# An MoE decoder trunk: experts' rows scattered to two rows per token and read back by plain loads

## The reference, cut to what matters

```
g_sel = argmax(g_logits)
e_in  = e_logits[token, g_sel]
top_v, top_i = top_k(e_in, 2)
top_w = softmax(top_v) * p_g
y     = sum over the two experts of top_w * (silu(x @ w_gate) * (x @ w_up)) @ w_down
x     = x + y
```

## Time and profile before

| | |
|---|---|
| median of 3 runs | 1473.19 us (1470.67 to 1476.38) |
| the profiled execution | 1473.54 us |
| its span, first to last instruction | 1471.9 us |
| PE busy | 1217.6 us (83%) |
| DVE, ACT, POOL busy | 371.1, 246.6, 230.0 us |
| moved by DMA | 350.99 MB, mean 238 GB/s |
| mean granted TensorE clock | 0.918 of full speed |

### The profile page before, as it was taken

How to read it: one execution, slowest core, us unless ns; L and a number is a source line. 1 busy time by engine, 2 the same in 40 slices (tenths; PEclk the granted TensorE clock), 3 DMA queues, 4 the chain that set the end, 5 groups by cost and what they waited for, 6 DMA issues and landing times.

```text
span 1471.9 us, 15943 instructions
## 1 busy us (share of the span) xinstructions
PE 1217.6 (83%) x6119; PEld 653.3 (44%) x6119; DVE 371.1 (25%) x808; ACT 246.6 (17%) x571; POOL 230.0 (16%) x288
## 2 busy tenths in 40 slices
PE   6999998888879689878855999997969679988770
PEld 4765574556534433333323764444734433333220
DVE  4132003544301511111114400112610531111115
ACT  2000005652201201100003201014410301000001
POOL 2300003222100011111022000303810011111103
PEclk9999999999999789989986999999969879999995
DMA  8320665749965669999948130302156659999955
GB/s 274 98 66 21 237 285 167 213 163 367 315 235 232 231 252 421 421 420 420 414 170 281 57 105 16 129 0 80 44 193 282 236 183 418 420 421 421 418 205 207
DMA packets 107725, 350.99 MB, mean 238 GB/s; under 512 B 21662, under 2 KB 40290, under 8 KB 84986
## 3 DMA queue, kind: packets, MB, share of 16 engines
q1 hardware_dynamic: 89880, 304.43, 54.1%
q0 software_dynamic: 17472, 45.37, 8.7%
q10 hardware_dynamic: 290, 0.07, 0.0%
HBM read 320.09 MB, written 44.41 MB: 248 GB/s over the span
## 4 chain that ended last, share of the span: by engine, by line
PE 58%; SPq 14%; DMA 8%; DVE 6%; issue 5%; POOL 4%; ACT 3%; POOLq 2%; DVEq 0%; ACTq 0%; PEldq 0%
SPq L1032 10%; PE ps L1222 9%; PE ps L1155 8%; PE ps L1726 8%; PE ps L436 4%; DMA moe_gu<-in_moe_w_up 4%; SPq L1054 4%; PE ps L1240 4%; PE ps L414 4%; PE ps L1677 4%; DMA fox_arena<-in_cache_k 2%; PE ps L355 2%; PE ps L694 1%; PE ps L1212 1%; PE ps L712 1%
## 5 line engine op out<-in xcount | busy, mean ns | idle before, releaser
L1222 PE MATMUL ps<-moe_gu,rows 128*64 128x512 f32 x1024 | 251.4, 648 | 58.3 <-DMA moe_gu<-in_moe_w_up 53.6
L1222 PEld LDWEIGHTS ps<-moe_gu,rows 128*64 128x64 f32 x1024 | 82.3, 149 | 204.9 <-issue 196.8
L1155 PE MATMUL ps<-moe_gu,turned 128*128 128x512 f32 x256 | 115.1, 613 | 12.4 <-DMA moe_gu<-in_fox_w_out 7.1
L1726 PE MATMUL ps<-mwblk,turned 128*128 128x512 f32 x256 | 111.5, 593 | 2.3 <-DVE vaug L1919 1.5
L1116 POOL DMA_INDIRECT expert_rows<-turned,moe_dst_row x32 | 32.0, 999 | 392.2 <-ACT turned L1327 384.6
L1494 DVE TENSOR_TENSOR turned<-turned,ps 128x256 f32<-128x256 f32 x32 | 13.5, 421 | 308.9 <-ACT turned L1317 308.9
L1155 PEld LDWEIGHTS ps<-moe_gu,turned 128*128 128x128 f32 x256 | 50.3, 198 | 76.2 <-issue 63.1
L1240 PE MATMUL ps<-moe_wd,moe_rowsel 128*64 128x512 f32 x352 | 80.4, 598 | 2.3 <-ACT turned L1327 2.3
L1726 PEld LDWEIGHTS ps<-mwblk,turned 128*128 128x128 f32 x256 | 48.0, 190 | 61.1 <-issue 57.4
L1317 ACT ACTIVATE turned<-ps 128x256 f32<-128x256 f32 x32 | 12.3, 383 | 318.0 <-PE ps L1222 318.0
L355 PE MATMUL ps<-turned,fox_arena 128*128 128x288 f32 x256 | 63.1, 407 | 0.0
(11 more groups left out here) (345 smaller groups left out, 1475.3 us busy)
## 6 DMA issues: line engine op xcount, KB each, us to landing
moe_gu<-in_moe_w_gate SPq DMA_DIRECT2D x56, 1024.0 KB, 22.7
moe_gu<-in_moe_w_up SPq DMA_DIRECT2D x56, 1024.0 KB, 24.3
moe_wd<-in_moe_w_down SPq DMA_DIRECT2D x44, 1024.0 KB, 23.0
rows<-in_moe_w_down SPq DMA_DIRECT2D x20, 1024.0 KB, 22.5
fox_arena<-in_cache_k SPq DMA_DIRECT2D x32, 512.0 KB, 7.7
fox_arena<-in_cache_v POOLq DMA_DIRECT2D x32, 512.0 KB, 9.5
fox_arena<-in_fox_w_in SPq DMA_DIRECT2D x6, 2048.0 KB, 10.1
expert_rows<-x SPq DMA_DIRECT2D x6, 2048.0 KB, 22.8
```

The source lines that it names most:

```text
L1155: mm = pe.matmul(ps[:, 2 * n + half, :], turned[:, c, n * P:(n + 1) * P], w[:, c, half * 512:half * 512 + 512], start=(c == 0), stop=(c == ...
L1222: mm = pe.matmul(ps[h, 2 + p % 2, :].rearrange("s (k f) -> s k f", k=2), xT[:, c, h], gu[s][:, half, :, c, :], start=(c == 0), stop=(c == ...
L1726: mm = pe.matmul(ps[:, m % 4, :], turned[:, c, n * P:(n + 1) * P], wblk[:, k % 3, c, :], start=(c == 0), stop=(c == KC - 1))
```

## The change

- `expert_rows` now has two rows per token (1,152 instead of 3,200). The destination of a pick is row 2 × token + j, j being 0 or 1. The fill is nine loads of 128 rows.
- The selection is in two passes. The first, for the experts' own tiles, compares the rank itself with the slot numbers (`rowsel`) and uses the one-hots over experts times the token's number, and times 2 × token + j, as `tilesel`; both are ready without floor, scan and sums. PE's ten pairs of products (32 columns) wait for all of them at once. One DVE instruction turns the result into source and destination rows (`row`). The second pass computes `tl` and `md` as before, for the 18 overflow tiles alone, with ten pairs of products (18 columns) and `more_row`. On PE it stands ahead of `turn_rows(0)`; on DVE it stands between `row` and `keep_turned(0)`.
- The one-hots of groups are no longer masked by `valid`; the products of ones for the last tile take 64 rows.
- After the experts SP waits for `scattered` and issues five plain loads, one per token tile, of two rows (8 KB) per partition, into `gu[0]` and `gu[1]`. This is still in `out_and_experts`. The ten gathers of `mlstm_project` and of `finish` are gone, and so is `slot`.
- `combine` waits for the tile's load and does both rows. In `finish` the mean of the tile before now stands behind both combinations, directly ahead of its end.
- SP's wait for six combinations ahead of the first block of projection weights is gone.

The diff, cut to its core:

```diff
@@ trunk
-        y_dram = nc.dram_tensor("expert_rows", (TILES * SLOT, D), F32, kind="Internal").ap()
+        y_dram = nc.dram_tensor("expert_rows", (2 * TOK, D), F32, kind="Internal").ap()
@@ fill_rows
+            for row in range(0, 2 * TOK, P):
+                sp.dma_start(y_dram[row:row + P, :], x[:, 0, :]).then_inc(filled, 16)
@@ out_and_experts
+            held = [gu[n // 4][:].rearrange("p h k c n -> p (h k c n)")[:, n % 4 * 2 * D:(n % 4 + 1) * 2 * D] for n in range(NT)]
@@ sp_ of out_and_experts, at its end
+                sp.wait_ge(scattered, 1)
+                for n in range(NT):
+                    sp.dma_start(held[n][0:ROWS[n], :], y_dram[2 * n * P:2 * (n * P + ROWS[n]), :].rearrange("(p j) d -> p (j d)", j=2)
+                                 ).then_inc(back_in[layer][n], 16)
@@ pool_ of out_and_experts
-                pool.wait_ge(index_ready, 2)
...
+                pool.sem_inc(scattered, 1)
@@ route
+                pe.wait_ge(sel_ready, 3)
                 for k in range(2 * NT):
-                    pe.wait_ge(sel_ready, k + 1)
                     for h in range(2):
-                        mm = pe.matmul(ps[h * SLOT:(h + 1) * SLOT, 2, 0:TILES // 2], rowsel[:, k, :], tilesel[:, k, h:TILES:2],
-                                       start=(k == 0), stop=(k == 2 * NT - 1))
+                        mm = pe.matmul(ps[h * SLOT:(h + 1) * SLOT, 2, 0:2 * STATIC].rearrange("s (u t) -> s u t", u=2), rowsel[:, k, :],
+                                       tilesel[:, k, :, h:EXP:2], start=(k == 0), stop=(k == 2 * NT - 1))
                 mm.then_inc(src_done, 1)
+                pe.wait_ge(more_ready, 1)
+                for k in range(2 * NT):
+                    for h in range(2):
+                        mm = pe.matmul(ps[h * SLOT:(h + 1) * SLOT, 3, 0:MORE].rearrange("s (u t) -> s u t", u=2), rowsel[:, k, :],
+                                       more_sel[:, k, :, h:MORE:2], start=(k == 0), stop=(k == 2 * NT - 1))
+                mm.then_inc(more_done, 1)
@@ routes
-                ch(dve.tensor_tensor(goh, goh, wide(const("valid"), GROUPS), ALU.mult))
...
-                    ch.step(dve.tensor_tensor(oh[:, j]...
+                    ch(dve.tensor_tensor(oh[:, j]...
+                dve.tensor_tensor(tilesel[:, :, 1, :], hot, back_row.broadcast_to([P, 2 * NT, EXP]), ALU.mult).then_inc(sel_ready, 1)
+                dve.tensor_tensor(tilesel[:, :, 0, :]..., oh, token.broadcast_to([P, 2, NT, EXP]), ALU.mult).then_inc(sel_ready, 1)
...
                 ch(dve.tensor_reduce(s10["r"][:], picked, AX, ALU.add))
+                dve.tensor_tensor(rowsel[:], numbers, rank.broadcast_to([P, 2 * NT, SLOT]), ALU.is_equal).then_inc(sel_ready, 1)
...
+                dve.wait_ge(src_done, 1)
+                dve.tensor_scalar(row[:].rearrange("s u t -> s (u t)"), ps[:, 2, 0:2 * STATIC], NOWHERE, None, ALU.add).then_inc(index_ready, 1)
...
+                ch.step(dve.tensor_tensor(rowsel[:], numbers, md.broadcast_to([P, 2 * NT, SLOT]), ALU.is_equal))
+                ch(dve.tensor_tensor(more_hit, ..., ALU.is_equal))
+                ch.step(dve.tensor_tensor(more_sel[:, :, 0, :]..., ALU.mult))
+                ch(dve.tensor_tensor(more_sel[:, :, 1, :], ..., ALU.mult))
+                dve.sem_inc(more_ready, 1)
...
+                dve.wait_ge(more_done, 1)
+                dve.tensor_scalar(more_row[:].rearrange("s u t -> s (u t)"), ps[:, 3, 0:MORE], NOWHERE, None, ALU.add).then_inc(index_ready, 1)
@@ combine
+        def combine(dve, layer, n, combined):
             r = ROWS[n]
+            dve.wait_ge(back_in[layer][n], 16)
+            for j in range(2):
+                if j:
+                    dve.wait_ge(combined, 2 * n + 1)
+                dve.scalar_tensor_tensor(x[0:r, n, :], back[layer][n][0:r, j * D:(j + 1) * D], share[j][0:r, n:n + 1], x[0:r, n, :], ALU.mult, ALU.add
+                                         ).then_inc(combined, 1)
@@ mlstm_project
-                sp.wait_ge(combined, 2 * NT - 4)
                 load_block(sp, 0)
...
-                for k in range(2 * NT):
-                    n, j = divmod(k, 2)
-                    gather_back(pool, yg[k][0:ROWS[n], :], n, j, yg_in[k])
@@ finish
-                for k in range(2 * NT):
-                    n, j = divmod(k, 2)
-                    gather_back(pool, yg[0:ROWS[n], k, :], n, j, yg_in[k])
...
-                    for j in range(2):
-                        k = 2 * n + j
-                        combine(dve, yg[0:ROWS[n], k, :], n, j, yg_in[k], 0, combined)
-                        if j == 0 and n:
-                            mean(dve, n - 1)
+                    combine(dve, 1, n, combined)
+                    if n:
+                        mean(dve, n - 1)
                     if n == 0:
                         dve.wait_ge(gl_in, 16)
                     else:
                         end(dve, n - 1)
```

More of the change, by code:

```diff
@@ L50 @@
           ("selpair", MPAIRS * P), ("iota_slot", SLOT), ("iota_tile", TILES),
-          ("rev4", GROUPS), ("rev32", EXP), ("token", NT), ("own_row", TILES // 2), ("valid", NT), ("minus_half", MH * NT), ("fold", LG)]
+          ("rev4", GROUPS), ("rev32", EXP), ("token", NT), ("back_row", 2 * NT), ("minus_half", MH * NT), ("fold", LG)]
 OFFSET, CW = {}, 0
@@ L89, in constants @@
     tok = np.arange(NT)[None, :] * P + i
-    c["valid"][:] = tok < TOK
     c["token"][:] = np.where(tok < TOK, tok - NOWHERE, 0)
-    c["own_row"][:] = np.arange(TILES // 2)[None, :] * P + i
+    c["back_row"][:] = np.concatenate([np.where(tok < TOK, 2 * tok + j - NOWHERE, 0) for j in range(2)], 1)
     c["minus_half"][:] = -0.5
@@ L161, in trunk @@
         half = sb("half", [P, 1])
-        slot = sb("slot", [P, 2, NT], U32)
         share = [sb(f"share{j}", [P, NT]) for j in range(2)]
@@ L181, in fill_rows @@
         def fill_rows(sp):
-            left = TILES * SLOT
-            while left:
-                n = min(left // P, NT - 1)
-                row = TILES * SLOT - left
-                sp.dma_start(y_dram[row:row + n * P, :].rearrange("(n p) d -> p n d", p=P), x[:, 0:n, :]).then_inc(filled, 16)
-                left -= n * P
+            for row in range(0, 2 * TOK, P):
+                sp.dma_start(y_dram[row:row + P, :], x[:, 0, :]).then_inc(filled, 16)
+        back_in = [[lasting(f"back_in{layer}_{n}") for n in range(NT)] for layer in range(2)]
+        back = []
         def log_sigmoid_act(act, neg_abs, e, u, lnu, bent, rounded, logged):
@@ L986, in out_and_experts @@
             both = sb(tag + "both", [P, NT + 1, EXP], where=mx)
-            c32 = {n: sb(tag + n, [P, EXP], where=mx) for n in ("ov", "end", "far")}
+            c32 = {n: wr[:].rearrange("p c s -> p (c s)")[:, 256 + k * EXP:256 + (k + 1) * EXP] for k, n in enumerate(("ov", "end", "far"))}
             rowsel = sb(tag + "rowsel", [P, 2 * NT, SLOT], where=mx)
@@ L1561, in mlstm_project @@
             HT = TOK // 2
-            vflat = vaug[:].rearrange("p n h v -> p (n h v)")
-            yg = [og[:, k, :] for k in range(NT)] + [vflat[:, k * D:(k + 1) * D] for k in range(NT)]
             hnorm = sb("hnorm", [P, D], where=small)
@@ L1583, in mlstm_project @@
             ss_done, qs_ready, gated = sem("m_ss"), sem("m_qs"), sem("m_gated")
-            combined, yg_in = sem("c0_combined"), [lasting(f"c0_yg_in{k}") for k in range(2 * NT)]
+            combined = sem("c0_combined")
             squared, meaned, rooted = sem("m_squared"), sem("m_meaned"), sem("m_rooted")
@@ L2394, in finish @@
             L = NT - 1
-            yg = sb("f_yg", [P, 2 * NT, D], where=fin)
+            sb("f_held", [P, 2 * NT, D], where=fin)
             gl = sb("gl", [P, D], where=fin)
-            combined, yg_in = sem("f_combined"), [lasting(f"f_yg_in{k}") for k in range(2 * NT)]
+            combined = sem("f_combined")
             gl_in, squared, meaned, rooted, ended, y_out = (sem("gl_in"), sem("f_squared"), sem("f_meaned"), sem("f_rooted"),
```

90 lines of the change are left out of this document (42 added, 48 removed).

## The result

| | before | after |
|---|---|---|
| median of the runs, us | 1474.22 (1470.67 to 1476.38) | 1460.50 (1458.48 to 1462.45) |
| ratio after/before, 95% interval | | 0.9913 (0.9891 to 0.9936) |
| profiled execution, its span, us | 1473.54, 1471.9 | 1459.13, 1457.4 |
| POOL: busy us, instructions | 230.0, 288 | 209.8, 268 |
| a second comparison | 1471.93 | 1460.39, ratio 0.9926 (0.9903 to 0.9950) |

The changed kernel is 13.7 us faster by the medians, 12.8 by the ratio; the second comparison gives 10.9 by its ratio and 11.5 by its medians. The forecast was 1463.9, with 1456 to 1471 as its range.

The account below looks back on a forecast made before the run. TensorE and the transfers were taken to bound the kernel in turns, the transfers inside the expert loop. From 1473.54 us, −6.3 − 5.2 − 1.6 + 3.5 = −9.6 gave 1463.9 us, range 1456 to 1471.

Parts of the forecast that it names:

- Routing: Rank product to transposes of gathered rows: transposes start 3.1 us earlier per layer, −6.3 for two layers (−4.2 to −8.0).
- Loop: Expert loop: scatters carry the same rows to other addresses and POOL issues as many, 0, bounds ±1.
- rival D: Expert loop: second selection and a slower stream eat the earlier start, loop ends as before; sum −3.3, 1470.2; chance 0.10.
- Phase end behind layer 0: After layer 0's experts: barrier earlier or later by SP's issues and POOL's drain, gate product at 788.75, −5.2 (−3.5 to −6).
- One of my signs: In the phases after the experts: no POOL instruction over 0.6 us, listed among what would show the forecast.
- POOL's drain: Projection's end and last phase's end: drain proportional to transfers POOL issued, ten gathers go, −1.6 (0 to −1.7).
- Last phase: After layer 1's experts: DVE waits for the final gain queued behind five loads, +3.5 (−3.9 to +5).
- rival B: Last phase: the gain does not stand behind the loads, −3.9 for +3.5; sum −17.0, 1456.5; chance 0.15.
- the term that was undersized: Last phase: five loads and the gain, 4.72 + 0.52 MB, take 3.73 + 4.72/0.4 = 15.5 us.
- The steps of 4.56 a tile: Last phase: each of four tiles takes two combinations, a mean, the openly awaited root and the end, 4.56 us.
- Rival C: Both phase ends after the experts: SP's drain waits for its five transfers; sum +7.5, 1481.0; chance 0.09.
- Fill: Start: row buffer's fill falls from 13.1 MB to 4.7 MB under a busy PE, 0.

Follow-up runs that it names:

- experiment 5: The kernel before with the two-pass routing alone; destinations, row buffer and gathers as before: 1463.55 us, ratio 0.9928.
- experiment 6: The changed kernel with TensorE's second selection moved behind the first expert tile's gate and up product: 1464.95 us, ratio 0.9938.
- Experiment 9: The changed kernel with the five row loads of each layer issued behind the barrier, at the start of the next phase: 1465.63 us, ratio 0.9944.
- experiment 10: The changed kernel with the final gain loaded early and the last phase's mean back between the two combinations: 1455.01 us, ratio 0.9880.
- experiment 7: The changed kernel with extra POOL drains, in each expert loop and before its wait at each phase end: 1452.43 us, ratio 0.9854.
- experiment 3: The changed kernel with SP loading the final gain ahead of the five row loads: 1452.45 us, ratio 0.9872.
- experiment 4: The changed kernel with the row buffer of 3,200 rows and its full fill of 13.1 MB: 1460.19 us, ratio 0.9922.

## Why the prediction was right

**Routing: −6.3 forecast, −6.3 measured.** The two numbers agree better than the terms do. The forecast had 0.2 a layer from the mask that goes, and 2.9 behind the rank product's reading. The mask's 0.2 did not come: with it gone the rank product, whose last tile now takes 64 rows, takes 2.48 us instead of 2.28 (2.29 in experiment 5, which keeps the old products), and from the logits' reading to the rank product's it is 10.7 us in both kernels. The rest came out at 3.2 instead of 2.9. The reading that mattered was that the gather, though issued 3.9 sooner, isn't what the transposes wait for: TensorE's second selection stands in front. The trace shows the transposes without a wait behind it. I had the first selection at 2.5, it took 2.35, and its lower bound of 2.1 did not come: the 2.36 of before was TensorE's own pace and not that of the ten DVE steps that fed it. Experiment 5 gives the same step alone (−2.7 to −3.0 a layer).

**Loop: 0.** 237.7 and 237.2 against 237.1: rival D is out (in layer 1 the loops, 238.9 to 241.1, scatter by more than the two kernels differ). What the first product starts sooner, the loop ends sooner; experiment 6 shows the same from the other side.

**Phase end behind layer 0: −5.2 forecast, −4.7 measured.** The barrier moved by 3.0, which is SP's issues (2.63) and its own drain (0.38). I had 2.4 for the issues and nothing for that drain, and 2.6 for both in the sum, 0.2 more than my terms give. The first rows were in time. Experiment 9 shows that the early issue is worth 1.4 of the 4.7, so the other 3.3 come from plain loads and a POOL that is free for the roots: the first root starts 5.5 us behind the barrier's memset in the changed kernel, and no gather stands before it (before: 780.24, 14.0 behind the memset at 766.29). One of my signs did not come: I wanted no POOL instruction over 0.6 us, and this root takes 1.53, beside a combination that began 0.17 us ahead of it. It is what experiment 10 found in the last phase, and it stood in the changed kernel's own trace (timeline):
```profile
767.37 2.59 DVE L1571 SCALAR_TENSOR_TENSOR x<-moe_gu,share,x 128x1024 f32<-128x1024 f32 x2
...
767.54 1.53 POOL L1681 TENSOR_TENSOR rstd<-ms,cst 128x1 f32<-128x1 f32 x1 [14.34 <-DVE ms L1846]
```

**POOL's drain: −1.6 forecast, −1.7 measured.** The proportionality to the transfers issued (2.71 for 32, 0.87 for 10, 0.06 for 0) was read from the four drains in the earlier trace rows; experiment 7 shows that it counts from POOL's last drain, not from the phase's start.

**Last phase: +3.5 forecast, +4.2 measured.** The mechanism held, and rival B with it fell: the gain lands behind the loads (7.98 us idle, gone in experiment 3). The Trainium skill ("DMA: Bandwidth & Descriptors", section "Queues, rings and completion order") states that each DMA engine consumes the descriptors of a ring in order; experiments 3 and 7 agree, with 16.4 us from the first load to the gain in two kernels that issued it at different times. That is the term that was undersized: 15.5 forecast, 16.4 measured. The first load, of 1 MB, landed 4.8 us behind its issue (5.0 by the term); the other 4.2 MB came at 360 GB/s, where I had 400. The steps of 4.56 a tile were 4.5. But the remedy that I drew from that term, a mean moved back between the combinations, was wrong as I put it ("the root that DVE now waits for openly ... before, the second combination lay over it"): the cover exists only when the root gets in first.

**Rival C** fell by one row: SP's drain takes 0.38 us with five loads in flight.

**Fill: 0 forecast, 0 measured** (experiment 4).

**Not forecast: the cells' phase,** 77.8 and 77.9 in two executions before and 75.1 to 76.4 in all that have the new routing, with or without the rest of the change. In the changed kernel its first masks waited 7.19 us for the loads of gate rows, in the repeat of before 8.56, and they start 11.3 and 11.0 us behind the phase's memset, against 12.7 and 12.6: that is 1.4 to 1.6 of the 2.0. Since experiment 5 has most of it, the loads, the buffer and the fill are not needed for it. Which part of the routing moves a later phase was not tried, and stays open. Without it the stretches sum to −8.5, 1 short of the forecast. That both medians (1460.50 and 1460.39) lie on the fast side of 1463.9 comes from what the forecast did not have, this phase and what is left in the attention's spread, and not from its terms: so far it is luck.

## What to carry to other kernels

A transfer issued behind others in one queue lands when they have: issue the small load that the end needs (here a gain of 0.5 MB) ahead of the 4.7 MB, which was worth 7.9 us, more than half of what this whole change gained. Count GpSimd's cost at a barrier by what it issued since it was last drained, and drain it where it has nothing to do for the next 10 us. And where VectorE and GpSimd both read SBUF, a cover can turn on a tenth of a microsecond between their starts; check the short instruction's duration in the trace and not only its place.

## What the runs showed of the hardware that I had not expected

- GpSimd's drain is paid per transfer that it issued since its last drain, 0.08 us each (2.7 for 32, 0.87 for 10, 0.23 for two), also long after they have landed; a drain in idle time makes the next one 0.06 us. Taking it from four barriers gave 8.0 us by the medians. With a transfer of its own in flight the drain lasted until 1.3 us behind the landing, 9.0 to 9.8 us. SP's drain took 0.38 us with five loads in flight.
- A wait that is already met, 0.08 us, in front of a VectorE instruction shortened a GpSimd instruction from 1.57 to 0.54 us and the tile from 4.24 to 3.80.
- Forty small products on TensorE cost 2.31 to 2.36 us from 9 to 32 columns. The same forty of 18 columns took 1.29 us directly behind a long product and 2.33 behind idle time. The granted clock is 1.00 (2.4 GHz) in the 2 us around the former (experiment 6) and one half, 1.2 GHz, in those around the latter (the changed kernel):
```profile
531.00:533.00 2.00, 2.00 (x47) 1.81 (x44) 0.60 (x2) 0.39 (x1) 0.00 (x0) 1.00 0.93 246
```
```profile
508.00:510.00 2.00, 1.03 (x20) 1.03 (x22) 1.78 (x5) 0.00 (x0) 0.85 (x1) 0.50 0.56 146
```
